# Residual boundaries: transposes in two halves between products, residual banks of two projections reordered, two weight splits on VectorE and one behind the copies

## The reference, cut to what matters

```
h = h + dsa_mixer(rms_norm(h, a_attn_norm[i]), ..., a_w_o[i], ...)        # ends in  out @ w_o     ("wo")
h = h + sq_relu_mlp(rms_norm(h, mlp_norm[layer]), w_up[layer], w_down[layer])   # "M0"
h = h + mla_mixer(rms_norm(h, b_attn_norm[j]), b_w_dq[j], ..., b_w_o[j], ...)   # "bo", then "M1"
x = x + merged @ w_out                                                    # "co"
x = x + (jax.nn.silu(hf @ w_gate) * (hf @ w_up)) @ w_down                 # "F", hf = rmsnorm(x)
```

## Time and profile before

| | us |
|---|---|
| median of 3 runs | 1141.1 |
| lowest and highest run | 1137.57, 1142.21 |
| profiled execution | 1141.42 |
| its span, first to last instruction | 1139.6 |
| its mean granted TensorE clock | 0.996 of full |

### The profile page before, as it was taken

The page is one execution under the profiler, slowest core; times in us unless marked ns, Lnnn a source line. Parts: engine busy times, 40 slices in busy tenths (PEclk is TensorE's granted clock), DMA queues, the critical chain, the costliest instruction groups (busy, mean ns, idle before and its releaser), DMA issues.

```text
span 1139.6 us, 17781 instructions
## 1 busy us (share of the span) xinstructions
PE 1112.0 (98%) x7033; PEld 984.8 (86%) x7033; DVE 707.6 (62%) x997; ACT 583.6 (51%) x767; POOL 142.6 (13%) x105
## 2 busy tenths in 40 slices
PE   8899999999998999999999999999999999999997
PEld 7767888888887888888888999898899989999996
DVE  5764565565668646565656878566587566554554
ACT  5565544444579554444455546455555346443443
POOL 3543300000265240000030000000000011000001
PEclk9999999999999999999999999999999999999999
DMA  7917565555442236556545654436643545656552
GB/s 216 306 54 186 182 198 188 200 190 184 118 137 88 98 111 222 191 186 201 189 156 185 204 171 149 132 128 223 203 159 120 185 148 160 221 175 194 189 172 89
DMA packets 138782, 193.96 MB, mean 170 GB/s; under 512 B 7147, under 2 KB 112840, under 8 KB 138716
## 3 DMA queue, kind: packets, MB, share of 16 engines
q1 hardware_dynamic: 126796, 181.92, 48.4%
q10 hardware_dynamic: 11312, 11.05, 3.6%
q0 software_dynamic: 608, 0.08, 0.1%
HBM read 191.90 MB, written 6.37 MB: 174 GB/s over the span
## 4 chain that ended last, share of the span: by engine, by line
PE 83%; ACT 6%; DVE 5%; issue 2%; DMA 2%; POOL 0%; ACTq 0%; DVEq 0%; POOLq 0%
PE psum L548 20%; PE psum L549 20%; PE psum L550 20%; PE psum L709 11%; PE psum L710 5%; ACT arena L1552 3%; PE psum L637 2%; ACT whi L1566 2%; DVE wlo L2125 1%; DMA raw<-in_a_w_in 1%; PE psum L1264 1%; PE psum L668 1%; PE psum L1237 1%; DVE arena L2566 1%; DMA raw<-in_b_w_o 0%
## 5 line engine op out<-in xcount | busy, mean ns | idle before, releaser
L1566 ACT ACTIVATE whi<-raw 128x2048 fp32r<-128x2048 f32 (+2 forms) x174 | 325.9, 1875 | 255.5 <-PE psum L550 172.5
L2125 DVE TENSOR_TENSOR wlo<-raw,whi 128x2048 fp32r<-128x2048 f32 (+1 forms) x149 | 337.5, 2267 | 184.1 <-ACT whi L1566 183.2
L548 PE MATMUL psum<-xA,whi 128*128 128x256 f32 x840 | 239.8, 285 | 2.7 <-DVE wlo L2125 1.7
L549 PE MATMUL psum<-xA,whi 128*128 128x256 f32 x840 | 237.6, 283 | 0.0
L550 PE MATMUL psum<-xA,wlo 128*128 128x256 f32 x840 | 237.5, 283 | 0.0
L1535 POOL TENSOR_TENSOR wlo<-raw,whi 128x288 fp32r<-128x288 f32 (+3 forms) x56 | 112.6, 2037 | 793.8 <-ACT whi L1566 793.5
L709 PE MATMUL psum<-xA,whi 128*128 128x512 f32 x512 | 183.0, 400 | 0.0
L548 PEld LDWEIGHTS psum<-xA,whi 128*128 128x128 f32 x840 | 160.3, 191 | 6.0 <-DVE wlo L2125 3.2
L549 PEld LDWEIGHTS psum<-xA,whi 128*128 128x128 f32 x840 | 160.4, 191 | 0.7
L550 PEld LDWEIGHTS psum<-xA,wlo 128*128 128x128 f32 x840 | 160.4, 191 | 0.1
L548 PE MATMUL psum<-whi,xC 128*128 128x512 f32 (+1 forms) x384 | 149.2, 389 | 1.1 <-DVE xC L2439 1.1
(11 more groups left out here) (269 smaller groups left out, 1339.7 us busy)
## 6 DMA issues: line engine op xcount, KB each, us to landing
raw<-in_w_in SPq DMA_DIRECT2D x42, 1024.0 KB, 4.9
raw<-in_mlp_w_up SPq DMA_DIRECT2D x32, 1024.0 KB, 5.4
raw<-in_mlp_w_down SPq DMA_DIRECT2D x32, 1024.0 KB, 4.8
raw<-in_w_gate SPq DMA_DIRECT2D x11, 1024.0 KB, 5.1
raw<-in_w_up SPq DMA_DIRECT2D x11, 1024.0 KB, 5.2
raw<-in_w_down SPq DMA_DIRECT2D x11, 1024.0 KB, 4.8
raw<-in_a_w_in SPq DMA_DIRECT2D x6, 1024.0 KB, 7.1
raw<-in_a_w_o SPq DMA_DIRECT2D x4, 1024.0 KB, 4.7
```

Source lines behind the costliest of these rows:

```text
L548: nc.tensor.matmul(out, lh, rh, start=start, stop=False, skip_group_check=skip)
L549: nc.tensor.matmul(out, lh, rl, start=False, stop=False, skip_group_check=skip)
L1566: nc.scalar.activation(whi[c % N_SPLIT][:, 0:n], raw[c % N_RAW][:, 0:n], ACT.Copy).then_inc(hi_sem, 1)
L2125: V.tensor_tensor(wlo[c % N_SPLIT][:, 0:n], raw[c % N_RAW][:, 0:n], f(whi[c % N_SPLIT][:, 0:n]), ALU.subtract).then_inc(lo_sem["dve"], 1)
```

## The change

- `late_transposes` does one half at a call. Half 0 stands between quarters 0, 2, 1 and quarter 3 of the last residual step (`last_residual_step`, and the end of `mlp`). Half 1 stands inside the next product: behind the tiles k = 0, 1 of both column tiles in M0, M1 and F (`first_tiles`), before k = 2 in B, before the second token block of the first part in C.
- DVE adds the quarters in the order 0, 2, 1, makes the low parts of k = 0, 1, then adds quarter 3.
- wo and bo write quarters 0 to 3 into banks 4, 3, 5, 2 where they wrote 2, 3, 4, 5, so that the up step's banks 4 and 5 are those of quarters 0 and 2.
- The low parts of wo2 and wo3 are made by DVE: wo2 behind `normed_out(L, 3)`, wo3 behind the mask casts and the turn table.
- ACT's split of dkva in B moves behind the first four copies. The split of qm0 in C (high and low) moves ahead of the norm's squares and means.

```diff
-            rows(f"wo{j}", kview(t["a_w_o"][0]), 2 * j, 2, D)
+            rows(f"wo{j}", kview(t["a_w_o"][0]), 2 * j, 2, D, lo="dve" if j > 1 else "pool")
...
-        res_base = {"wo": 2, "bo": 2}
+        res_banks = {"wo": (4, 3, 5, 2), "bo": (4, 3, 5, 2)}
...
+            def last_residual_step(tag, n, x, ready):
+
+                residual_step(tag, 3, x, ready, (0, 2, 1))
+                late_transposes(n, tag, 0)
+                residual_step(tag, 3, x, ready, (3,))
...
+            def first_tiles(n, tag):
+
+                ready = late_tile(n)
+                for k0 in range(0, KT, 2):
+                    if k0 == 2:
+                        late_transposes(n, tag, 1)
+                    for nt in range(2):
+                        for k in (k0, k0 + 1):
+                            if nt == 0:
+                                ready(k)
+                            yield nt, k
...
-                late_transposes(n, ("wo", "bo")[i])
...
-                up_step(c0, None, low[c0], 0, late_tile(n))
+                up_step(c0, None, low[c0], 0, first_tiles(n, tag))
...
-                down_step(c, b0 + NM, low[c], (NM - 1) % 3, False, True)
+                down_step(c, b0 + NM, low[c], (NM - 1) % 3, False, True, (0, 2, 1))
+                late_transposes("BC"[i], n, 0)
+                down_step(c, b0 + NM, low[c], (NM - 1) % 3, False, True, (3,))
...
+                    if kk == 2 and nt == 0:
+                        late_transposes("B", "M0", 1)
...
-            token_part("vm0", 0, (2, 3), late_tile("C"))
+            token_part("vm0", 0, (2, 3), late_tile("C"), lambda: late_transposes("C", "M1", 1))
...
-            wide_step(c0, low[c0], None, 4, late_tile("F"))
+            wide_step(c0, low[c0], None, 4, first_tiles("F", "co"))
...
-            split_to("dkva")
...
-                    if g and k == 3:
-                        split_to("dkvb")
+                    if k == 3:
+                        split_to("dkvb" if g else "dkva")
...
-            late_norm("C", "M1")
+            late_norm("C", "M1", index["qm0"])
...
-                for i in range(4):
+                for i in (0, 2, 1):
                     residual_add(tag, i)
                 for k in range(KT):
+                    if k == 2:
+                        residual_add(tag, 3)
...
                 normed_out(L, 3)
+                if L == "A":
+                    low_of("wo2")
                 out_low(L, 3)
...
+            low_of("wo3")
             mlp(0, "wo")
```

More of the change, by code:

```diff
@@ L587, in token_major, with down_products @@
                 chunk_done[c] = full[f"{name}.0"]
-            def down_products(c, xh, xl, start, stop, closing, skip=False, base=0, quarters=(0, 1, 2, 3)):
+            def down_products(c, xh, xl, start, stop, closing, skip=False, banks=(0, 1, 2, 3), quarters=(0, 1, 2, 3)):
                 hi, lo = slot(c, 2, D)
[L592 to L601, removed]
+                for quarter in quarters:
+                    blk, half = quarter // 2, quarter % 2
+                    for k in range(2):
+                        ins = three(psum[:, banks[quarter], :], xh(k, blk), xl(k, blk),
+                                    hi[:, k, half * 512:half * 512 + 512], lo[:, k, half * 512:half * 512 + 512],
+                                    start and k == 0, stop and k == 1, skip)
+                    if closing:
+                        close_bank(ins, closing[quarter])
                 return ins
@@ L616, in residual_step @@
                                     j == 0, j == 3, names if j == 3 else None,
-                                    base=res_base.get(tag, 0), quarters=quarters)
+                                    banks=res_banks.get(tag, (0, 1, 2, 3)), quarters=quarters)
                 if 3 not in quarters:
@@ L703, in up_step, with down_step @@
                     hi, lo = slot(c, KT, STEP)
-                    for nt in range(2):
+                    for nt, k in tiles or ((nt, k) for nt in range(2) for k in range(KT)):
                         out = psum[:, 4 + 2 * j2 + nt, :]
[L706 to L711, removed]
+                        nc.tensor.matmul(out, hi[:, k, nt * P:nt * P + P], xA[:, :, k, :], start=k == 0, stop=False)
+                        ins = nc.tensor.matmul(out[:, 0:SEQ], lo[:, k, nt * P:nt * P + P], xA[:, 0, k, :],
+                                               start=False, stop=k == KT - 1)
                     ins.then_inc(up_full, 1)
-                def down_step(c, h_count, lo_count, j3, start, last):
+                def down_step(c, h_count, lo_count, j3, start, last, quarters=(0, 1, 2, 3)):
                     pe.wait_ge(lo_sem[chunks[c]["lo"]], lo_count)
@@ L719, in down_step @@
                                         lambda k, blk: hb[:, 1, k, blk * P:blk * P + P],
-                                        start, True, names if last else None, True)
+                                        start, True, names if last else None, True, quarters=quarters)
                     if not last:
@@ L808, in attention @@
                 product(1, (3,))
-                for j in (2, 3):
-                    product(j, (0, 1, 2, 3))
+                product(2, (0, 1, 2, 3))
+                last_residual_step(tag, "M0" if L == "A" else "M1", xA, lambda j: read[f"{L}.oT{j}"])
             logit_bank = (4, 5, 2, 3)
@@ L1114, in _, with token_part @@
             mlp(1)
[L1117 to L1123, removed]
+            def token_part(name, part, banks, ready=None, between=None):
                 c = index[f"{name}{'ab'[part]}"]
@@ L1127, in token_part @@
                 for blk in range(NB):
+                    if part == 0:
+                        if blk and between:
+                            between()
+                        open_bank(f"{name}.{blk}", banks[blk])
                     for k in range(4):
```

61 lines of the change are left out of this document (28 added, 33 removed).

## The result

| | before | after |
|---|---|---|
| median, us | 1138.70 (20 runs) | 1143.66 (20 runs) |
| lowest and highest run | 1137.47, 1143.15 | 1139.52, 1152.0 |
| profiled execution | 1141.42 | 1145.45 |
| its span | 1139.6 | 1143.7 |
| its mean granted TensorE clock | 0.996 | 0.991 |

The ratio after to before is 1.0037, 95% interval 1.0022 to 1.0052: by this ratio the changed kernel is slower by 4.2 us, somewhere between 2.5 and 6 (the two medians lie 5.0 apart). That is under the half percent named ahead, and 1143.66 lies inside the range, but the forecast of about one us gained was wrong.

What follows compares the result with a forecast made beforehand. PE, busy 98%, bounds the kernel; its five boundaries lose 3.35 us together. +0.85 - 0.55 - 0.65 - 0.7 = -1.05 from the profiled 1141.42 gives 1140.4; predicted median 1140.2, range 1136.5 to 1144.5.

Steps and rivals of the forecast that it cites:

- The halves: Transposes in two halves at the boundaries recover PE stalls: M1 -0.55, B -0.65, C 0, F -0.7 us.
- the half copy's chain: From the half copy to d0's first product: 5.48 us, claimed to stay as it was.
- the 0.08 that I charged: Extra cost in us of each return of PE from transposes to products, now twice instead of once per boundary.
- dkva and qm0 behind other work: In B, 72 other products (8.6 us) hide dkva's later split; in C, 48 products (11 us) cover squares delayed by qm0.
- The first boundary: wo to M0: late loads of u0 and u1 put the up step at 124.3 and d0 at 136.7, +0.85 us.
- loads too late: Rival, 0.07: u0 flies beyond about 10.3 us, its low part holds PE; up to +5.75 in all, 1148.6 with half clock.
- I take 8.9: Assumed flight of u0's load in us, issued at 108.5: landed at 117.4, low part ready at 124.0.
- the 126 past which I had called it wrong: Sign at the first boundary: the forecast is wrong if POOL's row for u0 ends past 126; expected near 124.
- a wait of the longest kind: PE's wait if u0 flies 16.0 us: +7.65 at the first boundary, and half clock costing up to 1.7.
- The other warning sign: The forecast is wrong if the granted clock shows a new stretch at 0.50 in one of the boundaries.
- The clock by the transposes: Rival, 0.01: transposes among products count as idleness; each of five boundaries pays 1.7 us, 8.5 in all, 1149.
- Nothing gained at the halves: Rival, 0.14: returns, another tile wait and unmoved chains eat the 1.9 us; the first boundary costs 0.85: 1142.

Runs made afterwards that it cites:

- the wait filled: Changed kernel plus 14 multiplications of ones into an unused bank ahead of M0's up step: 1140.88 us, ratio 1.0009 to the kernel before.
- the splits alone: Kernel before with only the low parts of wo2 and wo3 moved to DVE: 1142.16 us, ratio 1.0007.
- the one with the copy earlier: Changed kernel with the copy into skew_c issued at head 8 of layer A instead of head 11: 1138.12 us, ratio 0.9988 to the kernel before.

## Why the prediction was wrong

**The halves: right.** Expected -0.55, -0.65, 0, -0.7; measured -0.69, -0.79, -0.05, -0.78. The steps held: no wait for tile 0, none for DVE's fourth addition, the half copy's chain unchanged. That three of them came out some 0.1 better is one small term. Eight transposes take 0.79 from start to start (417.21 to 418.00), where I had taken 0.88 from a row of the chain. The return to products costs 0.31 instead of 0.23 for the first, the 0.08 that I charged. So the up step of M1 starts 2.24 behind the first transpose instead of 2.32, and d0 12.36 behind that instead of 12.43. At M1, d0 came 14.60 behind the first transpose; I had said 14.8.

**dkva and qm0 behind other work: right for dkva, too small for qm0.** B's and C's boundaries show no cost of them. But I had written that qm0's split delays squares whose result is wanted only 48 products later; with half 1's late copies ahead of them too, the result came too late for two of the four norm products, 0.2 us.

**The first boundary: the mis-sized term.** I wrote +0.85 and it was +4.40. The mechanism was named, as the rival "loads too late", with its turning point at a flight of 10.3 us for u0; u0 flew 10.8. The step that failed is "I take 8.9", between the bounds 4.8 and 16.0, and what hung on it:

| part | predicted | measured |
|---|---|---|
| PE held at the up step | 1.4 | 3.46 (126.04 - 120.34, less 2.24 as at M1) |
| half clock behind it, with ACT's late chain to d0 | 0 | 1.6 (14.03 from up step to d0, against 12.43 with the wait filled) |
| gain of the halves there | -0.55 | -0.7 (as at M1) |
| sum | +0.85 | +4.4 |

u0 landed 1.8 us later than taken (119.2 for 117.4), and since PE had been 0.2 early the wait grew by 2.1. POOL's row ended at 125.8, just under the 126 past which I had called it wrong. The half clock I had charged only to a wait of the longest kind; a wait of 3.3 us was enough at this place, and one of 2.3 too (the splits alone). The length of a wait doesn't decide by itself, though: in B the 2.39 of the kernel before had no half clock behind it and the 1.70 of the changed kernel had. The size that I had for it, up to 1.7, was right: 1.5. The other warning sign that I named, a new stretch at 0.50 in a boundary, did show.

Why 8.9 was a poor choice: it was u1's flight of before, under another tail of skew_c, and I reasoned in bytes, that skew_c would lie across half of u0's flight only. By 108.5 the copy had moved 2.66 MB where I had read 2.30 before, so even less was left, 0.5 of 3.15 MB, and u0 still flew 10.2 to 10.9 us in four kernels with that order. Without skew_c it was 5.2. The DMA queues show how (q1 the loads, q10 skew_c; packets, MB, share), in the changed kernel from 110 to 114 us, then in the one with the copy earlier from 106.2 to 108.2:

```profile
q1 hardware_dynamic: 530, 0.54, 48.9%
q10 hardware_dynamic: 198, 0.20, 40.5%
```

```profile
q1 hardware_dynamic: 684, 0.70, 106.1%
```

Beside the copy the load moved 0.135 MB in a us, alone 0.35. And the copy itself slowed down, to 0.05 MB in a us from 0.19 between 100 and 104. So its last 0.5 MB lasted until 116 and not 115, and lay across 8 us of u0's 10.8. Working in proportion to the bytes that are left of the copy gives too little. The middle of the two bounds was 10.4, just past the turning point, and with the half clock priced at 1.5 the sum would have come out 1.7 above the kernel before.

**The clock by the transposes: fell.** The eight transposes of half 0 at M1, with the first product behind them, in the changed kernel:

```profile
417.20:418.10 0.90, 0.90 (x10) 0.89 (x9) 0.69 (x1) 0.26 (x1) 0.90 (x1) 1.00 1.03 423
```

The granted clock is 1.00, the 2.4 GHz level, and so it is at B, C and F and in half 0 of the first boundary. The stretch at half clock in the first boundary came as well with one block of 16 and went away with the transposes in halves and the wait filled. The Trainium skill, page "TensorE: Matmul & The Clock Gate", Part 4: PE-mode transpose, lets the full clock not engage for transposes; in this mix of products and transposes no run here shows that.

**Nothing gained at the halves: fell**, by the four boundaries above.

**The base and the range.** 1143.66 lies in the range by luck of the base. I started from 1141.1, the median of three runs; that of twenty is 1138.70. The same range around it would have ended near 1142. And 1140.4 less 0.3 is 1140.1, not 1140.2; nothing hangs on that.

**What stays open.** The boundaries together account for 4.4 - 2.3 = 2.1 us of the 4.2 that the ratio gives, whose lower bound is 2.5. Part of the rest may be the set of runs of the kernel before: its median was 1138.70 here and 1140.29, 1140.75 and 1141.55 beside the experiments, and against those three 1143.66 would be 2.1 to 3.4 more. Over the executions the mean granted clock is 0.9922 for the changed kernel and 0.9937 to 0.9945 for the kernel before in those three sets. That is one to one and a half stretches of 3.4 us at half (1.7 in 1140 is 0.0015), and one is already in the 2.1. What is left has no place in the one profile I have of each; u0 landing later in other executions would fit and isn't shown. Why the copy and the load together move fewer bytes (0.185 MB in a us) than the load alone isn't settled; that the copy's tail doubles u0's flight is shown by moving it both ways.

## What to carry to other kernels

When a step is moved to an idle engine, ask first what its end releases: here a low part, moved for 4.5 us of POOL, released a load 15 us later, and the load's chain became the path. Between far bounds for a load's flight take the middle or worse, find what other transfer lies across it, and move that transfer (to where loads have slack, not into a loop with two buffers) before giving up the change. An idle gap on PE like those here (1.7 to 3.3 us) may bring a stretch at half clock of another 1.5; price the change with it and without, and a profile tells which. Dummy products in the gap took it away here.

## What the runs showed of the hardware

- A load of 1 MB flew 5.2 us with skew_c out of the way, 10.2 to 10.9 issued when 0.5 MB of the 3.15 MB copy was left, 13.0 to 16.0 beside most of it, and 19.5 in one case with the copy inside M0's loop. Beside the copy a load moved 0.135 MB in a us, alone 0.35. u1 issued at 114.8 flew 5.1, issued at 113.0 it flew 10.5: later issue can mean earlier landing.
- At the first boundary, PE's idle gaps of 3.29 and 2.29 us were followed by 3.4 us at a granted clock of 0.51 and 0.50; gaps of 1.82 and 1.54 were not, and 14 multiplications of ones in the gap kept the clock at 1.00. In B a gap of 2.39 (before) was followed by none and one of 1.70 (after) by one.
- Eight transposes cost 0.79 us from start to start and sixteen 1.81 (121.92 to 123.73); the return to 512-wide products costs 0.08. So splitting a block of 16 in two cost nothing here.
